# SwiGLU up products as seven block products, with the down product spread between the pairs of inner tiles

## The reference

```python
for l in range(2):
    x = x + 0.5 * swiglu(rmsnorm(x, g_ffn1[l]), w1_a[l], w3_a[l], w2_a[l])
    x = x + merged_mixers(rmsnorm(x, g_mix[l])) @ w_o[l]     # Fourier, short convolution, pooling, gates
    x = x + 0.5 * swiglu(rmsnorm(x, g_ffn2[l]), w1_b[l], w3_b[l], w2_b[l])
return rmsnorm(x, g_final)

def swiglu(h, w1, w3, w2):            # w1, w3: 1024 x 2816, w2: 2816 x 1024
    return (jax.nn.silu(h @ w1) * (h @ w3)) @ w2
```

## Time and profile before

| | |
|---|---|
| median of three runs | 3089.13 us |
| profiled execution | 3089.77 us, span 3087.9 us |
| TensorE busy | 2961.9 us, 96% |
| TensorE weight loads | 2370.8 us, 77% |
| VectorE busy | 1701.5 us, 55% |
| ScalarE busy | 1270.0 us, 41% |
| GpSimd busy | 400.2 us, 13% |
| mean granted TensorE clock | 0.981 |

### The profile page before, as it was taken

One profiled execution on the slowest core, in us unless ns is written; L12 is line 12 of the kernel. 1 busy time (PEld: TensorE's weight loads), 2 busy tenths in 40 slices (PEclk: granted clock), 3 DMA queues, 4 the chain that ended last, 5 costly groups with the idle time before them and its releaser, 6 DMA issues.

```text
span 3087.9 us, 32343 instructions
## 1 busy us (share of the span) xinstructions
PE 2961.9 (96%) x12832; PEld 2370.8 (77%) x12832; DVE 1701.5 (55%) x1909; ACT 1270.0 (41%) x1531; POOL 400.2 (13%) x328
## 2 busy tenths in 40 slices
PE   8995999999959999999999999999999999999997
PEld 6674777777747888888888888888888878888886
DVE  6627888888875443366555443344434565544433
ACT  6723777777753332223233332233322333332221
POOL 3214000011002110010111110111100111111101
PEclk9996999999989999999999999999999999999999
DMA  5152999999952223222232223322232232322231
GB/s 201 59 188 92 339 352 351 351 352 353 351 191 75 96 96 93 92 92 94 95 98 96 96 96 94 97 96 96 94 95 89 89 99 94 102 92 97 95 96 58
DMA packets 126204, 446.41 MB, mean 145 GB/s; under 512 B 16096, under 2 KB 16608, under 8 KB 125792
## 3 DMA queue, kind: packets, MB, share of 16 engines
q1 hardware_dynamic: 118656, 422.37, 40.3%
q10 hardware_dynamic: 2208, 11.43, 0.9%
q0 software_dynamic: 5184, 10.50, 0.9%
HBM read 440.03 MB, written 12.58 MB: 147 GB/s over the span
## 4 chain that ended last, share of the span: by engine, by line
PE 83%; DVE 8%; issue 4%; ACT 3%; POOL 2%; DMA 1%; SPq 0%; DVEq 0%; ACTq 0%; POOLq 0%
PE bank L443 28%; PE bank L445 27%; PE bank L444 27%; DVE w_lo L1306 3%; ACT w_hi L766 2%; ACT xeT_hi L867 0%; DVE ye L1568 0%; DMA raw<-in_rec_in 0%; POOL mv L1130 0%; DVE hT_lo L1558 0%; DVE st L1376 0%; POOL w_lo L1095 0%; PE bank L449 0%; PE bank L629 0%; DVE zc L1767 0%
## 5 line engine op out<-in xcount | busy, mean ns | idle before, releaser
L1306 DVE TENSOR_TENSOR w_lo<-raw,w_hi 128x1024 fp32r<-128x1024 f32 (+3 forms) x538 | 670.8, 1255 | 473.1 <-ACT w_hi L766 470.4
L443 PE MATMUL bank<-xg_hi,w_lo 128*128 128x512 f32 x2112 | 836.5, 396 | 8.4 <-DVE xg_lo L1649 5.3
L445 PE MATMUL bank<-xg_hi,w_hi 128*128 128x512 f32 x2112 | 827.9, 392 | 0.0
L444 PE MATMUL bank<-xg_lo,w_hi 128*128 128x512 f32 x2112 | 826.6, 391 | 0.0
L766 ACT ACTIVATE w_hi<-raw 128x1024 fp32r<-128x1024 f32 (+3 forms) x548 | 561.9, 1031 | 486.6 <-PE bank L445 482.5
L443 PEld LDWEIGHTS bank<-xg_hi,w_lo 128*128 128x128 f32 x2112 | 397.8, 188 | 98.5 <-DVE xg_lo L1649 9.1
L445 PEld LDWEIGHTS bank<-xg_hi,w_hi 128*128 128x128 f32 x2112 | 397.5, 188 | 91.6
L444 PEld LDWEIGHTS bank<-xg_lo,w_hi 128*128 128x128 f32 x2112 | 397.8, 188 | 87.2 <-issue 1.7
L443 PE MATMUL bank<-g_hi,w_lo 128*128 128x512 f32 x928 | 365.1, 393 | 0.4 <-DVE g_lo L1674 0.4
L445 PE MATMUL bank<-g_hi,w_hi 128*128 128x512 f32 x928 | 363.1, 391 | 0.0
L444 PE MATMUL bank<-g_lo,w_hi 128*128 128x512 f32 x928 | 361.8, 390 | 0.0
(11 more groups left out here) (248 smaller groups left out, 2802.2 us busy)
## 6 DMA issues: line engine op xcount, KB each, us to landing
raw_more<-in_moe SPq DMA_DIRECT2D x264, 512.0 KB, 6.1
raw<-in_moe SPq DMA_DIRECT2D x120, 512.0 KB, 6.1
raw<-in_w_a SPq DMA_DIRECT2D x120, 512.0 KB, 3.3
raw<-in_w_b SPq DMA_DIRECT2D x120, 512.0 KB, 3.3
raw<-in_w_in SPq DMA_DIRECT2D x88, 512.0 KB, 3.3
raw<-in_rec_in SPq DMA_DIRECT2D x20, 512.0 KB, 4.1
raw<-in_w_o SPq DMA_DIRECT2D x16, 512.0 KB, 3.3
raw<-in_w_a SPq DMA_DIRECT2D x16, 384.0 KB, 3.1
```

Of the source, the lines that this page charges most:

```text
L443: e.matmul(out, a_lo, b_hi, start=start, stop=False)
L444: e.matmul(out, a_hi, b_lo, start=False, stop=False)
L445: return e.matmul(out, a_hi, b_hi, start=False, stop=stop)
L1306: e.tensor_tensor(lo, raw_of(k), hi.bitcast(F32), ALU.subtract).then_inc(s["lo"], 1)
```

## The change

**The products.** The weight of an up product is seen as 2 x 2 blocks (k tiles 0 to 3 and 4 to 7; inner tiles j and j + 11), and h as 2 x 2 blocks (k tiles, and tokens 0 to 255 and 256 to 511). The 2 x 2 block product is computed with seven block products in place of eight, in Winograd's form. Each product is four k tiles by three matmuls, now of 256 columns. For this, sums of weight blocks and of h blocks are made first:

- weight_sums on VectorE: four sums of 512 columns for each of w1 and w3 in each pair. They give the operands S (a new buffer), D (in place in the load of the second tile) and E (in place in the load of the first).
- finish on VectorE and ScalarE: for each two tiles of xT, seven half tiles of xf_hi and xf_lo (xf has 7 x 256 columns for each of four k). Four subtractions or additions of half tiles, four high halves, four low halves.
- take on ScalarE: three copies of PSUM accumulators into SBUF (snap) for each weight and pair; first_corner, last_corner, up_first and up_second on VectorE subtract them, multiply by rsq, and multiply Silu(u) with v, which GpSimd did.

**The inner layer.** It now has 11 pairs (UP = 11). From pair 2 to pair 9 two weight chunks of the down product follow each pair on TensorE (down_part): four output tiles, each 4 k tiles x 3 = 12 matmuls of 512 columns. So a chunk of four hidden tiles is used up over two pairs, and each output tile is added to xT by a residual five times (CHUNKS = 5) in place of once. down_last does the last six hidden tiles. g_hi and g_lo shrink from 22 to 8 tiles.

**Banks.** The ring of seven stays for the other stages. In a SwiGLU banks are given by name: X and Y take banks 0, 1 and 4, 5 in turn (Y of a pair takes the banks that X of the pair before had), Z banks 2 and 3, the down tiles 6 and 7.

**Split buffers.** LOOK goes from 2 to 3, NSPLIT from 3 to 4, NMORE from 11 to 9; one more load buffer (NLATE = 1) serves the second block. These hold for all stages.

```diff
-LOOK = 2
-NRAW, NMORE, NSPLIT = 5, 11, 3
+LOOK = 3
+NRAW, NMORE, NLATE, NSPLIT = 5, 9, 1, 4
@@ weight_table
+            for j in range(UP):
+                for m, w in enumerate(("w1", "w3")):
+                    for h in range(2):
+                        fetch(("up", i, j, m, h), (0, io[f"{w}_{name}"][l, j + h * UP], W))
+                for kind in ("AB", "S", "D"):
+                    for m in range(2):
+                        block((kind, i, j, m))
+                if 2 <= j < 2 * CHUNKS:
+                    for q in range(2 * (j % 2), 2 * (j % 2) + 2):
...
@@ bank_table
+                for m in range(2):
+                    use(("X", n, m), "c21", 2 * n + 1 + m, x_banks(n)[m])
+                for m in range(2):
+                    use(("Y", n, m), "c11", 2 * n + 1 + m, x_banks(n + 1)[m])
...
+                        use(("dn2", i, j // 2 - 1, pos), "res", res_count(i, 8 * (j // 2 - 1) + pos), 6 + pos % 2)
@@ tensor_program, up_pair for j > 0 (each m: w1, w3)
+                        terms(xs[m], hi, lo, 0, ks, True, True).then_inc(s["pr"], 1)
...
+                        b = free_bank(("Y", n, m))
+                        terms(b, hi[:, T:W], lo[:, T:W], 1, ks, True, True).then_inc(s["pr"], 1)
...
+                    terms(xs[m], hi[:, T:W], lo[:, T:W], 4, ks, False, True).then_inc(s["pr"], 1)
...
+                    b = free_bank(("Z", n, m))
+                    terms(b, hi, lo, 3, ks, True, True).then_inc(s["pr"], 1)
...
+                    terms(xs[m], hi, lo, 5, ks, False, True).then_inc(s["pr"], 1)
...
+                    terms(bank_of(("Z", n, m)), e_hi[:, m, :], e_lo[:, m, :], 2, ks, False, True).then_inc(s["pr"], 1)
...
+                    terms(xs[m], hi[:, T:W], lo[:, T:W], 6, ks, False, True).then_inc(s["pr"], 1)
@@ vector_program, the order of a pair
             def swiglu(i):
+                p = ff_pass(i)
+                weight_sums(i, 0, 1)
+                for j in range(UP):
+                    n = UP * i + j
+                    last = at["D", i, j, 1]
+                    low(at["S", i, j, 1])
+                    if j in (1, 2):
+                        up_first(n - 1)
+                    first_corner(n)
                     if j == 0:
                         root(p)
+                    low(last)
+                    if j in (1, 2):
+                        up_second(n - 1)
+                    low_e(n)
+                    if j in (1, 2):
+                        up_split(n - 1)
+                    low(last + 2)
+                    last_corner(n)
+                    if j < 2:
+                        weight_sums(i, j + 1, 0)
+                        weight_sums(i, j + 1, 1)
+                    else:
+                        low(last + 4)
+                        up_first(n)
+                        c, half = j // 2 - 1, 4 * (j % 2)
+                        if j < UP - 1:
+                            weight_sums(i, j + 1, 0)
+                            down(i, 8 * c + half)
+                            up_second(n)
+                            down(i, 8 * c + half + 1)
+                            weight_sums(i, j + 1, 1)
+                            down(i, 8 * c + half + 2)
+                            up_split(n)
+                            down(i, 8 * c + half + 3)
+                        else:
+                            up_second(n)
+                            up_split(n)
```

More of the change, by code:

```diff
@@ L416, in sync_program @@
                 e.dma_start(hs[:, 2 * n:2 * n + 2, :], io["xT"][:, 2 * n:2 * n + 2, :]).then_inc(s_xt[n], 16)
-            for c in range(1, NCH):
-                load(c)
+            for k in range(1, len(loads)):
+                load(k)
             for j in range(DT):
@@ new lines, in down_terms, with down_part @@
+            def down_terms(b, hi, lo, col, first, count, start, stop):
+                for k in range(count):
+                    a = slice(col + k * P, col + (k + 1) * P)
+                    g = first + (k if count == 4 else 2 * k)
+                    f = mm3(b[:, :], hi[:, a], lo[:, a], g_hi[:, g, :], g_lo[:, g, :],
+                            start and k == 0, stop and k == count - 1)
+                return f
+            def down_part(i, c, q):
+                hi, lo = weights(("w2", i, c, q))
+                if q == 0:
+                    e.wait_ge(s["glo"], GLO_FF[i] + 4 * c + 4)
+                for h in range(2):
+                    b = free_bank(("dn2", i, c, 2 * q + h))
+                    down_terms(b, hi, lo, h * T, 4 * (c % 2), 4, True, True).then_inc(s["used"] if h else s["wt"], 1)
@@ L981, in root @@
+            finish(0, DT - 1, "ftd", DT // 2)
             def root(p):
@@ new lines, in swiglu @@
+                    high(last)
+                    high_e(n)
+                    take(n, "X", 5, 1)
+                    if j in (1, 2):
+                        up_split(n - 1)
+                    take(n, "Z", 7, 2)
+                    high(last + 2)
+                    if j >= 2:
+                        high(last + 4)
+                        up_act(n)
+                        up_split(n)
+                for n in range(DT):
+                    if n == 0:
+                        high(at["w2", i, CHUNKS - 1, 3])
+                    elif n == 2:
+                        high(at["w2", i, CHUNKS, 1])
+                    elif n >= 4:
+                        weights(at["w2", i, CHUNKS, 1] + n - 7)
+                    finish(p + 1, n, "res", res_count(i, 8 * (CHUNKS - 1) + n))
@@ L1297, in vector_program, with low @@
             made = [0]
-            def weights(c):
-                while made[0] <= min(c + LOOK, NCH - 1):
+            def low(c):
+                while made[0] <= min(c, NCH - 1):
                     k = made[0]
@@ new lines, in swiglu @@
+                for n in range(DT):
+                    if n == 0:
+                        low(at["w2", i, CHUNKS - 1, 3])
+                    elif n == 2:
+                        low(at["w2", i, CHUNKS, 1])
+                    elif n >= 4:
+                        weights(at["w2", i, CHUNKS, 1] + n - 7)
+                    if n == 6 and i % 2 and i + 1 < 2 * LAYERS:
+                        weight_sums(i + 1, 0, 0)
+                    down(i, 8 * (CHUNKS - 1) + n)
+                    finish(p + 1, n, "res", res_count(i, 8 * (CHUNKS - 1) + n))
```

791 lines of the change are left out of this document (549 added, 242 removed).

## The result

The changed kernel takes 3165.37 us (median of four runs, 3163.73 to 3167.34) against 3089.14 for the kernel before in the same session: 1.0247 times as long, 95% interval 1.0229 to 1.0265. It is slower, as forecast, by 76 us where 40 were forecast; the profiled execution has a span of 3161.9 us.

A forecast was written before the change was run, and what follows sets the result against it. TensorE was taken as the bound, with VectorE's queue order deciding the stalls. 3089.8 + 34 (SwiGLUs) + 5 (allowance) + 11 (first entry) - 9 (experts) - 1 (recurrence) = 3130 us; range 3105 to 3150, outer 3065 to 3180.

The forecast's parts named there:

- Products at 0.1178 us: SwiGLU up products: 256-column matmuls start 0.1178 us apart, so a pair's products go from 21.96 to 19.79 us.
- The steady stall: Pairs with down tiles: third down tile waits 2.65 us for residual 0 on VectorE; no second stall at tile 4.
- The period: One steady SwiGLU pair: 30.8 us of TensorE work plus the stall, 33.4 us against 32.94 before; 0.15 us allowance besides.
- rival (d): Clock falls to 1.2 GHz after each steady stall: 32 x 2.3 = 74 us more, 3204 us; chance 0.05.
- Pairs 0 to 2: First pairs of each SwiGLU: stalls of 4.3 us in pair 0, 3.0 and 2.5 us in pairs 1 and 2.
- The entries: First SwiGLU entry, without matmuls beside it, +11 us (bounds 5 and 17); late forms stall 0.9 us per SwiGLU.
- The experts, -9 us: Experts stage: deeper split buffers save 9 us (bounds -20 and +8), at most 20 us with DMA engines 96 to 97% busy.
- the recurrence: Recurrence stage: the deeper split buffers were taken to save 1 us.
- The sum: Whole kernel: 3130 us from 3089.8; own range 3105 to 3150 (chance 0.58), outer range 3065 to 3180.
- rival (c): VectorE's chain is longer by a microsecond a period, with full durations: 3162 us; chance 0.12.
- Rival (a): TensorE stays the bound: with residual 0 and corners always in time only the products count, 2995 us; chance 0.07.
- Rival (b): Half the stalls: each steady stall 1.3 us, experts gain all 20 us, 3076 us; break-even stall 2.17 us; chance 0.18.

The follow-up runs named there:

- experiment 4: Changed kernel with 12 more matmuls of 512 columns in each pair with down tiles, where TensorE waits for the bank: 3132.33 us, ratio 1.013.
- experiment 3: Changed kernel with the first two residuals ahead of the first four weight sums and the third ahead of the last four: 3062.14 us, ratio 0.9899.
- Experiments 2: Changed kernel with only the residual of each pair's first down tile put ahead of the first four weight sums on VectorE: 3160.74 us, ratio 1.023.
- experiment 5: Changed kernel with up_first, up_second and up_split of pairs 0 and 1 at the end of their own pair: 3184.0 us, ratio 1.0303.
- experiment 8: On experiment 3, only the root of pair 0 moved behind the low halves of D and E on VectorE and ScalarE: 3054.62 us, ratio 0.9884.
- experiment 10: On experiment 3, weight sums 32 columns wide in place of 512 except in a SwiGLU's first pair, so sums are incomplete: 3041.35 us, ratio 0.9844.
- experiment 1: Kernel before with LOOK 3, NSPLIT 4 and 14 load buffers in the experts (3 elsewhere), nothing else: 3054.16 us, ratio 0.9875.

## Why the prediction was right or wrong

- **Products at 0.1178 us.** Right, though the distance is not one number. From 1758.98 on the matmuls of 256 columns start 0.113 us apart (with those of E, at 0.12, that is 19.2 us for the products of a pair). So it is in 11 of the 36 later pairs of the changed kernel, in 28 of 36 in experiment 4, and in none in experiment 3. In the others it is 0.116 to 0.119, about 19.7 us, and the half microsecond shows in the periods: 32.8 and 33.4, 34.3 and 34.9. What sets the pace is not known. Two starts of experiment 3, 36 distances apart:

```profile
1707.74 0.28 PE L587 MATMUL bank<-xf_hi,w_lo 128*128 128x256 f32 x1
...
1711.98 0.28 PE L587 MATMUL bank<-xf_hi,w_lo 128*128 128x256 f32 x1
```

- **The steady stall: 2.65 us for tile 3, none for tile 4.** Right in place, cause and size: 2.34 us of idle TensorE plus the restart. Experiments 2 and 3 show the reason, the order of VectorE's queue; experiment 3 also refutes the volume theory for these pairs.
- **The period, 33.4 us and 0.15 of allowance.** 33.2 on average where the clock stayed, 34.3 over all. The missing term is rival (d), to which I gave 0.05 and 2.3 us a pair: the clock does fall after a wait of 2.3 us, though not after every one, and a fall costs 1.5 us (34.7 against 33.2). Experiment 4 gives 1.4 to 1.7 us a pair on average, some 46 us in all. It was wrong to hold (d) against the trace because short pauses had left the clock alone: the trace had no gap of that size in dense work, so it could not speak against it.
- **Pairs 0 to 2.** In SwiGLU 1 the waits were 1.00 before S (forecast 1.3), 1.79 and 2.10 before D and Z (forecast 2.0 in all), 3.13 in pair 1 (3.0), 0.61 + 3.12 in pair 2 (2.5), 2.85 at the exit (3.0). The order was read rightly. But I took each as a loss by itself. In SwiGLU 1 a wait removed comes back in a later product, more than all of it in experiment 5 and a good half in experiment 8, and what returned in one piece in experiment 5 is longer and took the clock with it. That is what a surplus of VectorE's work would do; experiment 10 agrees with it but cannot prove it.
- **The entries.** The first was forecast at +11 us and took 14. The entry of SwiGLU 2, which follows another SwiGLU, was given the same 0.9 us for late forms as those behind the mixers; there the forms cost 5.84 us.
- **The experts, -9 us.** This step failed: it is -38.0, outside its own bounds of -20 and +8, and the recurrence, given -1, is another -5.5. The working had the right size in it: 37 us by the DMA queue's cycle against 35 us of matmuls, for each of 16 pairs of experts, is 32 us. I cut it down because I took the DMA share of 97% for a ceiling. With the same loads at 373 GB/s the share is 99%, so it does not say what is left. The two load buffers less, for which I took off more, cost nothing that shows: experiment 1 has 14 too and gains 35 us of total time.
- **The sum.** 3130 against 3165: experts and recurrence were 33 us better than forecast, the SwiGLUs with the first entry 64 us worse (50 forecast, 114 measured), most of it the clock, and the mixers 4 us worse. Two errors of opposite sign partly cancel. That left the time inside the outer range of 3065 to 3180, though not inside the forecast's own 3105 to 3150; this part is luck. It came out next to rival (c), 3162, but not by (c)'s cause: VectorE's chain was not longer than counted.
- **Rival (a)**, 2995 us, says that only the products count if the residuals come in time. In experiment 3 they do, and it takes 3062: the waits of pairs 0 to 2, of the exits and of the entries stay. **Rival (b)** named the steady stall as the point from which the sign turns. In experiment 3, without that stall, the sign against the kernel before does turn, but only with the gain at the experts; beside experiment 1 it is 8 us slower.

The fastest kernels that leave nothing out are experiment 1 (3054.16) and experiment 8 (3054.62), the first with eight products. With the order mended, seven products are worth nothing that could be measured beside the same split depth. In the trace of experiment 8 the 95 us go four ways: TensorE idles 55 us more than before in the four SwiGLUs, in the first pairs, the exits and the entry of SwiGLU 2; the granted clock of 0.98 to 0.99 there is worth about 20 us, an estimate; the first entry takes 14 us more and the mixers 4.

## What to carry to other kernels

When TensorE is the bound and a change pays with VectorE's time, add up VectorE's queue in its order, not only its volume: find each instruction that frees a bank and count what stands ahead of it. Free the bank first, and do preparatory work after. Where another engine has more work than the bound one over a few steps, expect a mended wait to come back, at least in part, at the next step; here two waits of 4.5 and 4.7 us cost more than nearly the same idle time in shorter pieces. Compare stages at the same instruction in each kernel. And time a change of buffer depths by itself before it is counted with anything else.

## What the runs showed of the hardware

- A pause of 2.34 us in otherwise dense matmuls was followed by about 3 us at 1.2 GHz in 23 of 32 cases (granted clock 0.50 in 1752 to 1754), and not in nine others at the same place in the program: periods of 32.8 to 33.4 and of 34.2 to 35.7 us stand beside each other. 12 repeated matmuls in each pause made the kernel 33 us faster.
- DMA engines that were 96 to 97% busy at 348 to 357 GB/s moved 369 to 382 GB/s at 98 to 100% with LOOK 3 and four split buffers (experiment 1 and the changed kernel, 330 to 800 us).
- Matmuls of 256 columns with new weights each start 0.113 us apart in some pairs and 0.116 to 0.119 in others of the same kernel, with the clock at 1.00 in both.
